# One-hots of the product-key gates in groups of eight tokens, compared whole on VectorE and multiplied by GpSimd and ScalarE

## The reference

```
for token t, slot s (128 of them):  key0[t,s], key1[t,s] in 0..127,  gate[t,s]
G[t][a, b] = sum over s of  (key0[t,s] == a) * gate[t,s] * (key1[t,s] == b)
y[t] = sum over experts (a, b) of  G[t][a, b] * gelu(x[t] . u[a, b]) * v[a, b]
```

## Time and profile before

| | us |
|---|---|
| runs of the kernel before, median of three | 3048.86 (3037.66 to 3049.27) |
| the profiled execution, whole time | 3049.46 |
| its span (first to last instruction) | 3047.7 |
| the changed stage in it, first comparison to last copy | 99.2 (522.9 to 622.1) |
| busy in the stage: PE, DVE, ACT, POOL | 75.3, 87.9, 91.6, 0.0 |

### The profile page before, as it was taken

How to read it: one execution, slowest core, us unless ns; L and a number is a source line. 1 busy time by engine, 2 the same in 40 slices (tenths; PEclk the granted TensorE clock), 3 DMA queues, 4 the chain that set the end, 5 groups by cost and what they waited for, 6 DMA issues and landing times. The chain is left out here.

```text
span 3047.7 us, 41495 instructions
## 1 busy us (share of the span) xinstructions
PE 2578.3 (85%) x15802; PEld 1815.3 (60%) x15802; DVE 1176.9 (39%) x2448; ACT 683.7 (22%) x1268; POOL 58.9 (2%) x80
## 2 busy tenths in 40 slices
PE   5696887779999999988967699998956786999886
PEld 2273764679999999975846455444435554554442
DVE  2253087956666666643532411111135314111112
ACT  0031001944444444432211110000013111000000
POOL 0000000000000000000200000000000000000000
PEclk9857898999999999998988799999978897999998
DMA  5302332035555555556224189999941332999995
GB/s 184 131 1 83 125 124 95 0 131 185 187 188 183 192 181 192 182 187 211 74 84 187 56 341 427 426 427 426 413 156 46 141 143 106 428 426 427 427 427 244
DMA packets 128469, 654.65 MB, mean 215 GB/s; under 512 B 15312, under 2 KB 17104, under 8 KB 93392
## 3 DMA queue, kind: packets, MB, share of 16 engines
q1 hardware_dynamic: 115424, 625.64, 52.0%
q10 hardware_dynamic: 12912, 27.15, 2.5%
HBM read 643.97 MB, written 8.78 MB: 214 GB/s over the span
## 5 line engine op out<-in xcount | busy, mean ns | idle before, releaser
L428 PE MATMUL banks<-weight_ring,window_rows_T 128*64 128x256 f32 x2496 | 286.9, 384 | 45.6 <-DMA weight_ring<-in_moe_w_up 28.6
L428 PE MATMUL banks<-peer_input_high,u_high 128*128 128x256 f32 x1024 | 290.8, 284 | 14.4 <-DVE u_low L1070 14.4
L428 PE MATMUL banks<-peer_input_high,u_low 128*128 128x256 f32 x1024 | 291.1, 284 | 0.0
L428 PE MATMUL banks<-peer_input_low,u_high 128*128 128x256 f32 x1024 | 291.0, 284 | 0.0
L2366 DVE COPY expert_hidden_T<-banks 128x256 f32<-128x256 f32 x64 | 27.2, 425 | 678.2 <-PE banks L2228 678.2
L428 PEld LDWEIGHTS banks<-weight_ring,window_rows_T 128*64 128x64 f32 x2496 | 188.9, 138 | 157.5 <-issue 42.9
L428 PEld LDWEIGHTS banks<-peer_input_high,u_high 128*128 128x128 f32 x1024 | 197.2, 193 | 20.2 <-DVE u_low L1070 15.4
L428 PE MATMUL banks<-v_high,gated_high 128*128 128x512 f32 x512 | 201.1, 393 | 0.0
L428 PE MATMUL banks<-v_low,gated_high 128*128 128x512 f32 x512 | 201.0, 392 | 0.0
L428 PEld LDWEIGHTS banks<-peer_input_low,u_high 128*128 128x128 f32 x1024 | 197.2, 193 | 4.7
L428 PE MATMUL banks<-v_high,gated_low 128*128 128x512 f32 x512 | 199.4, 390 | 0.0
(11 more groups left out here) (453 smaller groups left out, 3589.3 us busy)
## 6 DMA issues: line engine op xcount, KB each, us to landing
weight_ring<-in_moe_w_down SPq DMA_DIRECT2D x42, 2048.0 KB, 35.4
weight_ring<-in_moe_w_gate SPq DMA_DIRECT2D x40, 2048.0 KB, 35.4
weight_ring<-in_moe_w_up SPq DMA_DIRECT2D x38, 2048.0 KB, 34.4
u_of_key<-in_peer_u_T SPq DMA_DIRECT2D x128, 512.0 KB, 4.2
v_of_key<-in_peer_v_rows SPq DMA_DIRECT2D x128, 512.0 KB, 3.5
more_weight_slots<-in_moe_w_up SPq DMA_DIRECT2D x26, 2048.0 KB, 33.9
more_weight_slots<-in_moe_w_gate SPq DMA_DIRECT2D x24, 2048.0 KB, 35.3
more_weight_slots<-in_moe_w_down SPq DMA_DIRECT2D x22, 2048.0 KB, 35.4
```

Source lines behind the costliest of these rows:

```text
L428: return k.nc.tensor.matmul(out, lhsT, rhs, start=start, stop=stop)
```

## The change

The groups have eight tokens (32 of them), with three buffers of one-hots. PE uses all eight PSUM banks, two for a group, so a bank pair comes round every four groups. DVE makes either side of a group with one comparison of 128x1024, both as plain one-hots. The multiplication by the gates is now wholly outside DVE: POOL multiplies five tokens of side 1 in one instruction of 128x640, in place, and ACT the other three as before. PE waits for both. ACT copies a group out in two instructions. The hardware loops are gone: all 32 groups are written out on every engine.

```diff
-    GRP = 4
-    BUF = 4
+    GRP, BUF = 8, 3
+    POOL_GATED = 5
+    groups = S // GRP
...
+            @block.gpsimd
+            def _(pool):
+                for g in range(groups):
+                    pool.wait_ge(k.onehots_ready.sem, k.onehots_ready.at(g + 1))
+                    mine = hot[:, g % BUF, 1, 0:POOL_GATED, :]
+                    nc.gpsimd.tensor_tensor(
+                        mine, mine,
+                        slots_T[:, 2, g * GRP:g * GRP + POOL_GATED].unsqueeze(2).to_broadcast([P, POOL_GATED, P]),
+                        ALU.mult).then_inc(k.pool_onehots.up(), 1)
...
             @block.vector
             def _(dve):
...
+                for g in range(groups):
+                    tok = slice(g * GRP, (g + 1) * GRP)
+                    if g >= BUF:
+                        dve.wait_ge(k.products.sem, k.products.at(g - BUF + 1))
+                    for side, sig in ((1, k.onehots_ready), (0, k.more_onehots)):
+                        nc.vector.tensor_tensor(hot[:, g % BUF, side, :, :],
+                                                slots_T[:, side, tok].unsqueeze(2).to_broadcast(sh),
+                                                iota[:, :].unsqueeze(1).to_broadcast(sh),
+                                                ALU.is_equal).then_inc(sig.up(), 1)
 
             @block.tensor
             def _(pe):
...
+                for g in range(groups):
+                    pe.wait_ge(k.more_onehots.sem, k.more_onehots.at(g + 1))
+                    pe.wait_ge(k.onehots_gated.sem, k.onehots_gated.at(g + 1))
+                    pe.wait_ge(k.pool_onehots.sem, k.pool_onehots.at(g + 1))
+                    if g >= 4:
+                        pe.wait_ge(k.gates_placed.sem, k.gates_placed.at(2 * (g - 4) + 2))
+                    for t in range(GRP):
+                        last = mm(k, k.ps[:, 2 * (g % 4) + t // 4, t % 4 * P:(t % 4 + 1) * P],
+                                  hot[:, g % BUF, 0, t, :], hot[:, g % BUF, 1, t, :])
+                    last.then_inc(k.products.up(), 1)
...
+                def scale(g):
+
+                    act.wait_ge(k.onehots_ready.sem, k.onehots_ready.at(g + 1))
+                    for t in range(POOL_GATED, GRP):
+                        mine = hot[:, g % BUF, 1, t, :]
+                        ins = nc.scalar.activation(mine, mine, ACT.Copy,
+                                                   scale=slots_T[:, 2, g * GRP + t:g * GRP + t + 1])
+                    ins.then_inc(k.onehots_gated.up(), 1)
...
+                scale(0)
+                for g in range(groups):
+                    if g + 1 < groups:
+                        scale(g + 1)
+                    place(g)
```

More of the change, by code:

```diff
@@ L250, in __init__ @@
         self.onehots_gated = signal("onehots_gated")
+        self.pool_onehots = signal("pool_onehots")
         self.gates_placed = signal("gates_placed")
@@ L890, in peer_gates @@
         load_small(k, [(iota[:, :], k.const("iota")[:, 0:PK])])
-        turns = S // GRP // BUF
         with k.stage() as block:
@@ L938, in _ @@
             @block.vector
             def _(dve):
[L940 to L946, removed]
+                sh = [P, GRP, P]
+                for g in range(groups):
[7 more added lines that the diff above has]
+                                                ALU.is_equal).then_inc(sig.up(), 1)
@@ L957, in _ @@
             @block.scalar
             def _(act):
[L959 to L968, removed]
@@ L969, in _ @@
-                place(act, BUF * turns - 1, BUF - 1)
+                def scale(g):
[5 more added lines that the diff above has]
+                    ins.then_inc(k.onehots_gated.up(), 1)
@@ new lines, in place @@
+                def place(g):
+                    act.wait_ge(k.products.sem, k.products.at(g + 1))
+                    for i in range(2):
+                        nc.scalar.activation(gates[:, :, g * GRP + 4 * i:g * GRP + 4 * i + 4],
+                                             k.ps[:, 2 * (g % 4) + i, :].rearrange("p (t n) -> p n t", t=4),
+                                             ACT.Copy).then_inc(k.gates_placed.up(), 1)
+                scale(0)
[3 more added lines that the diff above has]
+                    place(g)
```

## The result

The changed kernel took 3056.78 us (median of 20 runs, 3047.12 to 3063.63), the kernel before, on the same chip, 3048.49 (20 runs, 3037.14 to 3055.60). The ratio is 1.0025, with a 95% interval of 1.0014 to 1.0037: 7.6 us more, between 4.3 and 11.3. That is slower, but within the half per cent that the prediction called no change. I had forecast 19.4 us more.

A forecast was written before the change was run, and what follows sets the result against it. DVE and POOL taking turns on the SBUF port bound the stage: 1.14 + 1.08 + 1.36 = 3.58 us per group, 32 groups plus tail 118.6 us against 99.2, so 3049.5 + 19.4 = 3069 us, range 3053 to 3086.

The forecast's parts named there:

- The section on what would show it: Expected profile signs: stage about 118.6 us, step 3.6, DVE rows well over 1.22 us or POOL's well over 1.5.
- rival D: Stage's turns: POOL gives up the port some 0.35 us earlier, 11.2 us off, 3058 us; chance 0.11.
- A: Main case: DVE and POOL take turns on the SBUF port, 3.58 us per group, 3060 to 3080 us; chance 0.70.
- collision (3): In the earlier trace, a 64-element DVE copy took 2.235 us instead of 0.188, until POOL's multiply was over.
- The handover of 0.14 us: Between DVE and POOL, the second waits for the whole of the first, less 0.14 us.
- DVE, 1.14 us behind itself and 1.22 alone: Each 128x1024 comparison takes 1.22 us, stepping 1.14 behind another; two make 2.27 us per group.
- POOL's multiply: POOL's 128x640 multiply in each group was taken as 1.50 us, between 1.47 and 1.54.
- rival C: POOL's multiply slower because its gate input repeats one value innermost; at 1.9 us, 3082 us; chance 0.10.
- No price for a first call on POOL: The skill's about 6 us for a first GpSimd call was not added, as the trace did not bear it out.
- The tail: End of stage after the last turn: POOL's end, PE's release, last eight matmuls 2.35 us, ACT's wait and two copies.
- B: No turn-taking in the stage: DVE is the bound, stage 77.2 us, 22 us less, 3027 us; chance 0.09.
- E: PE at half clock in the stage: at worst 3 us and a last group 1 us slower; no chance of its own.

The follow-up runs named there:

- the kernel with the row pattern: Changed kernel with POOL's second input the row of key numbers, repeated per token, instead of the gates: 3067.49 us, ratio 1.0058 to the kernel before.

## Why the prediction was right in its mechanism and wrong in its size

**What bounds the stage: right.** The three instructions of a group take turns, half of DVE's rows are longer by about a microsecond and all of POOL's are. The section on what would show it had named one or the other; both at once was its sign for rival D, if with a step below 3.3 us, and the step is 3.33. It took the experiments, not that sign, to tell A from D. Taking the collision away (one input in PSUM) or taking POOL away gives the same 76 us. So the rule that I cited from the Trainium skill ("SBUF — State Buffer", Who interferes with whom) holds here in both directions: it names two SBUF inputs on VectorE as the condition, and with only one there was no turn-taking.

The prediction's own evidence for that condition was weaker than it says. Its collision (3) was of a DVE copy, which has one input, and that in SBUF: it waited all the same. So two inputs in SBUF are what made these comparisons wait, and not the only thing that can make a DVE instruction wait; no run here says which others do.

**The handover of 0.14 us: right.** It was read off two collisions. Three lengths of the multiply fit it: 1.14 + 1.08 plus the multiply's own length less 0.14 gives 2.91 for 0.83 us, 3.34 for 1.26 and 3.61 for 1.53, and the steps were 2.90, 3.33 and 3.61. (The steps fix only the sum of the two handovers of a turn, 0.28.)

**DVE, 1.14 us behind itself and 1.22 alone: right.** The comparisons alone step at 2.27 for two.

**POOL's multiply: the step that failed.** The term of the turn that was too long is the price of the multiply: "I take 1.50", from the bounds of 1.47 and 1.54, and in rival C "nothing makes it faster than 1.47". It took 1.256. I had seen that no row of POOL has a second input that repeats one value innermost, and allowed for it only on the slow side. The bounds were those of another pattern, and right for that one. (The fixed part of 0.2 in the upper bound does not follow from the copy's 0.61 us; the multiplies alone later gave 0.19.) Over 32 groups it is 32 x (1.50 - 1.256) = 7.8 us of the 8.5 by which the stage came out shorter than forecast (118.6 - 110.1). The nearest row was near in size, not in pattern, and that gave no reason to exclude a gain. With this term open downwards, "no change" would have had far more than its quarter.

The Trainium skill gives one price for such a two-input operation on POOL, in "GPSIMD Engine Reference", section 3.1: about 2.6 cycles an element, and no other where an input repeats one value. At the 1.2 GHz of that section this is an estimate of 2.17 ns. The slope measured with the row, 2.10 ns, is near it; the slope with the gate, 1.67, is not. The prediction's estimate from that section's 4497 ns, 1.55 us for 640 elements, was right for the row (1.53) and, like my 1.50, too long for the gate.

**No price for a first call on POOL: right.** POOL's first multiply began at 525.42, behind DVE's first comparison (from 524.12, 1.22 long), so no first call of some microseconds lies between them.

**The tail: 3.5 us, not 4.0.** The last eight matmuls took 2.02 us, not the 2.35 of the earlier trace rows, whose sixteen rows are two groups with a wait of their own each; eight behind one wait take less. That is most of the 0.5 us. ACT then began its copies 0.04 us after PE's recorded end (633.12, then 633.16), not 0.16; against that, PE started 0.26 us behind POOL's end, not 0.2.

**The kernel before as the mark: an effect that I didn't separate.** I summed the new stage from the bottom and took the old one as given, so the loops' price was in the sum, but not seen. Against the kernel before with its loops written out, the change costs 110.1 - 91.0 = 19.1 us; 8.2 come back because the loops go. What reads as a loss of 10.9 us is a loss by collision of 34 (110.1 against 76.1), over a gain of 23 (99.2 to 76.1). Of that gain 8.2 belong to the form of the loops. The other 15 are what is left: larger comparisons, and a lighter ACT (busy 88 of the 91 us in the kernel before with its loops written out, 62 of 76 in the kernel with one input in PSUM); no run takes these two apart.

**From the stage to the whole.** The whole came out 11.8 us below the forecast difference (19.4 against 7.6): 8.5 in the stage, 3.3 outside it. The stage lost 10.9 us and the whole 7.6 (4.3 to 11.3); they agree within the interval. The remaining 3 us aren't explained. Executions of one kernel differ by more than that, with the granted clock over the whole span: of the kernel before, beside the first experiments, from 3045.42 us at 0.925 to 3056.84 at 0.919. Why the kernels with written-out loops came out some 2 to 5 us lower as a whole than their stages say (and one, once, 11) stays open; what lies behind the stage took between 2416 and 2426 us in the profiles, so single profiles don't place it.

**The rivals.** B (no turn-taking, a stage of 77.2 us) was false as to the cause, and its number was about right for a stage without collisions: 76. (Its tail of 4.2 us is 3.95 by its own terms.) C was looked for on the wrong side. D named a time near the measured one, 3058, for a reason that the multiply by itself and the kernel with the row pattern rule out. E had no part: the granted clock of the stage stayed at 0.97.

## What to carry to other kernels

When work is moved to an idle engine, ask first by which way its operands come: here two engines with room to spare took 3.33 us in turns for what took 2.27 side by side, and one small operand moved to PSUM was worth 34 us. Take the price of an instruction from a row with the same access pattern, not only the same size; where there is none, leave both sides open. Before a new stage is compared with an old one, ask what the old one pays for its form (here 8.2 us for hardware loops), since a rewrite gives that back whatever else it does.

## What was new about the hardware

- POOL's multiply of two SBUF inputs is faster when the second input repeats one value in its innermost dimension: 1.67 ns an element against 2.10, with a fixed part of some 0.19 us either way. DVE's comparison took 1.23 us with its repeated row in SBUF (POOL left out) or in PSUM (POOL beside it).
- An instruction that waits for the other engine's SBUF reads is recorded as running: 2.17 us for 1.26 of work, 2.27 for 1.22. Such a wait can't be seen among the idle times or the waits; it shows as two durations of one form of instruction, in the minimum, median and maximum.
- Neither engine was starved. The order was DVE, DVE, POOL in each turn: at the end of an undisturbed comparison the way went to POOL, which had been waiting, though DVE's next instruction was issued before that end (563.04, against 563.11). In the rows shown, the one issued first goes first: POOL (562.06) ahead of DVE (563.04).
- Work that hides and work that collides look alike in the sums: POOL's 40 us of multiplies cost 0.1 us with one of DVE's inputs in PSUM, and 34 us with both in SBUF.
